# Gate values by indexed one-word transfers into a DRAM table, and a new order of the expert products

## The reference, cut to what matters

```
sc = q . sub_keys                          # 256 tokens, 8 heads, 2 halves, 128 keys
v1,i1 = top16(sc[half 0]);  v2,i2 = top16(sc[half 1])
top_s, pos = top16(v1[a] + v2[b])          # 16 experts of 16384 for a token and head
idx = i1[a]*128 + i2[b];  g = softmax(top_s)
out[t] = sum over 8*16 chosen experts k of  g[t,k] * gelu(x[t] . u[idx]) * v[idx]
```

## Time and profile before

| | us |
|---|---|
| device time, median of 2 runs | 1510.88 (1507.37 and 1514.4) |
| profiled execution: device time | 1509.89 |
| profiled execution: span, first to last instruction | 1508.1 |
| PE busy | 1470.0 (97%) |
| DVE / ACT / POOL busy | 889.2 / 819.0 / 576.4 |
| moved from and to HBM | 242.50 MB read, 7.34 MB written |

### The profile page before, as it was taken

How to read it: one execution, slowest core, us unless ns; L and a number is a source line. 1 busy time by engine, 2 the same in 40 slices (tenths; PEclk the granted TensorE clock), 3 DMA queues, 4 the chain that set the end, 5 groups by cost and what they waited for, 6 DMA issues and landing times.

```text
span 1508.1 us, 24377 instructions
## 1 busy us (share of the span) xinstructions
PE 1470.0 (97%) x8923; PEld 1302.1 (86%) x8923; DVE 889.2 (59%) x2185; ACT 819.0 (54%) x1483; POOL 576.4 (38%) x200
## 2 busy tenths in 40 slices
PE   7999999999999999989999999999999999999998
PEld 6788888788889898889999998888888888887886
DVE  4935259388336431225996662666666666667776
ACT  5556454488456644443556664555555555555554
POOL 6881665700467477456888884000000000000000
PEclk9999999999999999999999999999999999999999
DMA  8740435600334335333665334555555555556774
GB/s 332 274 169 29 167 129 177 225 30 2 108 121 163 140 141 183 121 143 113 197 211 153 98 105 161 196 195 194 185 185 189 193 195 195 186 189 219 243 241 163
DMA packets 60125, 251.08 MB, mean 166 GB/s; under 512 B 6144, under 2 KB 18560, under 8 KB 44160
## 3 DMA queue, kind: packets, MB, share of 16 engines
q1 hardware_dynamic: 60032, 249.86, 47.9%
HBM read 242.50 MB, written 7.34 MB: 166 GB/s over the span
## 4 chain that ended last, share of the span: by engine, by line
PE 66%; POOL 2%; ACT 2%; DVE 1%; issue 1%; DMA 0%; DVEq 0%; ACTq 0%
PE bank L1297 23%; PE bank L1321 9%; PE bank L702 6%; PE bank L869 6%; PE bank L1324 5%; PE bank L1250 4%; PE bank L705 3%; POOL wlo L1364 2%; PE bank L822 2%; PE bank L764 1%; PE bank L805 1%; ACT whi L1421 1%; PE bank L724 1%; PE bank L998 1%; PE bank L1150 1%; PE bank L980 1%
## 5 line engine op out<-in xcount | busy, mean ns | idle before, releaser
L1364 POOL TENSOR_TENSOR wlo<-raw,whi 128x2048 fp32r<-128x2048 f32 (+1 forms) x51 | 195.3, 3840 | 159.0 <-ACT whi L1421 158.7
L1364 POOL TENSOR_TENSOR wlo<-arena,whi 128x2048 fp32r<-128x2048 f32 (+1 forms) x45 | 195.1, 4342 | 151.1 <-ACT whi L1421 150.9
L1297 PE MATMUL bank<-whi,ghi 128*128 128x512 f32 x512 | 201.4, 393 | 3.6 <-DVE glo L2559 1.7
L1297 PE MATMUL bank<-wlo,ghi 128*128 128x512 f32 x512 | 201.0, 393 | 0.0
L1297 PE MATMUL bank<-whi,glo 128*128 128x512 f32 x512 | 200.0, 391 | 0.0
L1321 PE MATMUL bank<-hT,whi 128*128 128x512 f32 x624 | 154.3, 390 | 1.6 <-ACT whi L1767 1.6
L1321 PEld LDWEIGHTS bank<-hT,whi 128*128 128x128 f32 x624 | 117.0, 188 | 26.0 <-ACT whi L1767 1.8
L2516 DVE TENSOR_TENSOR wlo<-raw,whi 128x1024 fp32r<-128x1024 f32 x84 | 102.8, 1225 | 56.6 <-ACT whi L1774 56.6
L1377 POOL TENSOR_TENSOR wlo<-raw,whi 128x1024 fp32r<-128x1024 f32 x52 | 123.8, 2391 | 28.2 <-ACT whi L1717 28.1
L1421 ACT ACTIVATE whi<-arena 128x2048 fp32r<-128x2048 f32 x41 | 78.4, 1915 | 94.4 <-PE bank L822 28.7
L822 PE MATMUL bank<-whi,hT 128*128 128x512 f32 x512 | 125.8, 393 | 0.0
(11 more groups left out here) (336 smaller groups left out, 3027.0 us busy)
## 6 DMA issues: line engine op xcount, KB each, us to landing
raw<-ex_in SPq DMA_DIRECT2D x52, 1024.0 KB, 4.8
raw<-w_in SPq DMA_DIRECT2D x44, 1024.0 KB, 5.2
arena<-w_in SPq DMA_DIRECT2D x44, 1024.0 KB, 5.1
raw<-ex_in SPq DMA_DIRECT2D x84, 512.0 KB, 3.9
xw<-ex_in SPq DMA_DIRECT2D x26, 1024.0 KB, 4.7
xw<-ex_in SPq DMA_DIRECT2D x16, 512.0 KB, 4.0
arena<-spill SPq DMA_DIRECT2D x48, 128.0 KB, 3.8
spill<-gact SPq DMA_DIRECT2D x32, 128.0 KB, 3.7
```

Of the source, the lines that this page charges most:

```text
L1297: last = mm(bank[2 * t + h][:, :], g[:, j % 2, tok], w[:, b, at], start=False, stop=(final and i == 2), skip_group_check=True)
L1364: last = G.tensor_tensor(wlo[:, u % 2, at], slots[u % RING][:, at], whi[:, u % 2, at], ALU.subtract)
```

## The change

Stages 2 to 4 are replaced. No one-hot arrays, no transposes of the selection, no `spill`.

- **Table.** W lies in DRAM as `table` (128 tiles x 128 rows x 256 tokens, one fp32 word each, 16.8 MB). SP writes zeros to it with 16 transfers of 1 MB, four at a time, behind the loads of weight units 19, 45, 63 and 79.
- **Scatter.** DVE computes for each token and slot the place of its word. POOL issues, for each of the two token tiles, 128 indexed transfers of 128 words (one a partition). From slot 16 on they add to what is there, and after every 16 POOL waits until all issued have landed.
- **Units.** The work is a list of 356 units of 512 KB: `first` (the u of a tile) and `second` (the v of a tile, for one or both token halves). Tiles 0 to 99: first only. Tiles 100 to 127: each first is followed by a second of token half 0 of tile 0, 1, ..., 27. Then 72 seconds of half 0 (tiles 28 to 99). Then 25 times: one second of both halves (tiles 100 to 124) and four seconds of half 1; at the end three seconds of both halves. So the v of 100 tiles is loaded and split twice.
- **Ring.** All units share one ring of four quarters (raw, high, low). The first 16 low parts are POOL's, the others DVE's. On DVE they are put between the steps of the selection, by a count of spent time. The activations of all 128 tiles stay in SBUF; their gate values come back from the table through a ring of four.
- **Order on DVE.** Six of the eight score blocks come first, then the selection of token tile 0, then two score blocks and the selection of token tile 1. ACT's exponentials stand behind tiles 7 and 29.

```diff
-NL = 2 + XBODY * 13
-NA = N_KEYS - NL
+POOL_LOWS = 16
+MERGED = 48
+VISITS_FROM = 100
+VISITS = 100
+EXP_AT = (7, 29)
+UNITS = []
+for tile in range(N_KEYS):
+    UNITS.append(("first", tile, ()))
+    if visits_after(tile):
+        UNITS.append(("second", visits_upto(tile) - 1, (0,)))
+EARLY = VISITS
+UNITS += [("second", tile, (0,)) for tile in range(visits_upto(N_KEYS - 1), EARLY)]
+NARROW = 4
+for tile in range(EARLY, N_KEYS):
+    UNITS.append(("second", tile, (0, 1)))
+    if (tile - EARLY) * NARROW < EARLY:
+        UNITS += [("second", (tile - EARLY) * NARROW + i, (1,)) for i in range(NARROW)]
...
 SP:
+                if u in ZERO_AT:
+                    for i in range(4):
+                        sp_.dma_start(zero_rows[n], zeros_8).then_inc(zeroed, 16)
...
+            for n in range(NU):
+                if n < 4: ...
+                elif n - 4 < POOL_LOWS:
+                    sp_.wait_ge(u_lo_pool, n - 3)
+                else:
+                    sp_.wait_ge(u_lo_dve, n - 3 - POOL_LOWS)
+                sp_.dma_start(quarters[n % 4], ...).then_inc(u_loaded[n % 4], 16)
+                if n - 1 in PLACE:
+                    for t in some:
+                        sp_.wait_ge(scattered[t], 16 * SLOTS)
+                    if m >= 4:
+                        sp_.wait_ge(g_ready, m - 3)
+                    sp_.dma_start(w_ring[m % 4][:, tokens_of(m)], tiles_w[tile][:, tokens_of(m)])
...
 POOL:
+            pool.wait_ge(zeroed, 16 * 16)
+            for t in range(TT):
+                pool.wait_ge(places_ready, t + 1)
+                if t > 0:
+                    pool.wait_ge(scattered[0], 16 * SLOTS)
+                for s in range(SLOTS):
+                    if s > 0 and s % 16 == 0:
+                        pool.wait_ge(scattered[t], 16 * s)
+                    G.indirect_dma_start(table, IndirectOffsetOnAxis(ap=places[:, t, s:s + 1], axis=0),
+                                         values[:, t, s:s + 1], None, compute_op=ALU.add if s >= 16)
...
 PE:
+            for n in range(NU - 2):
+                if kind == "first":
+                    first_product(n, tile)
+                else:
+                    second_ready(n)          # waits glo_ready and the low part of v
+                    for t in some:
+                        last = out_part(n, t, False)
+                    last.then_inc(u_done, 1)
...
 ACT:
+            def unit_hi(n):
+                act.wait_ge(u_loaded[n % 4], 16 * (n // 4 + 1))
+                act.wait_ge(u_done, n - 3)
+                A(hi4[n % 4], quarters[n % 4], ACT.Copy).then_inc(u_hi, 1)
+            for n in range(NU - 2):
+                act.wait_ge(u_done, n + 1)
+                if first: copy of the second bank half (or gelu, tile < 48)
+                unit_hi(n + 4)
+                if first and tile >= MERGED: gelu, after DVE's sum
+                if n + 2 in PLACE:
+                    act_hi(PLACE[n + 2])     # ghi of unit n + 2
...
 DVE:
+            for n in range(lows[0] - 4, NU - 2):
+                if kind == "first" and tile >= MERGED:
+                    V.tensor_tensor(out, out, act_at(tile), ALU.add)
+                if n + 4 < NU:
+                    unit_lo()                # waits u_hi of unit n + 4, then 128x1024
+                if n + 2 in PLACE:
+                    act_lo(PLACE[n + 2])     # glo of unit n + 2
+                if n + 3 in PLACE:
+                    weigh(PLACE[n + 3])      # activation times gate, unit n + 3
```

More of the change, by code:

```diff
@@ L29, with visits_after, visits_upto @@
 PH = 8
-XRING = 3
-XBODY = 6
-NL = 2 + XBODY * 13
-NA = N_KEYS - NL
[L34 to L55, removed]
+SLOTS = PH * 16
+POOL_LOWS = 16
[3 more added lines that the diff above has]
+EXP_AT = (7, 29)
+def visits_after(i):
+    return 1 if i >= VISITS_FROM else 0
+def visits_upto(i):
+    return max(0, i - VISITS_FROM + 1)
+UNITS = []
[5 more added lines that the diff above has]
+UNITS += [("second", tile, (0,)) for tile in range(visits_upto(N_KEYS - 1), EARLY)]
+FIRSTS = len(UNITS)
+NARROW = 4
[3 more added lines that the diff above has]
+        UNITS += [("second", (tile - EARLY) * NARROW + i, (1,)) for i in range(NARROW)]
+NU = len(UNITS)
+SECONDS = [n for n, (kind, _, _) in enumerate(UNITS) if kind == "second"]
+PLACE = {n: m for m, n in enumerate(SECONDS)}
 SCALE = HD ** -0.5
@@ L144, in build @@
         x = xw[:, :].rearrange("p (t n) -> p t n", t=TT)
[L145 to L152, removed]
+        quarters, hi4, lo4 = ([w[:, i // 2, D * (i % 2):D * (i % 2) + D] for i in range(4)] for w in (raw, whi, wlo))
+        places = xw[:, 0:2 * SLOTS].bitcast(U32).rearrange("p (t n) -> p t n", t=TT)
+        values = xw[:, 2 * SLOTS:4 * SLOTS].rearrange("p (t n) -> p t n", t=TT)
+        expert, place, unread = (xw[:, (4 + i) * SLOTS:(5 + i) * SLOTS] for i in range(3))
+        w_ring = [xw[:, D + T * i:D + T * i + T] for i in range(4)]
+        token_u, token_f = sc8[:, 96:98].bitcast(U32), sc8[:, 98:100]
+        table = nc.dram_tensor("table", (P * N_KEYS * T, 1), FP32, kind="Internal").ap()
         slots = [raw[:, 0, :], raw[:, 1, :], arena[:, 0:UNIT], arena[:, UNIT:2 * UNIT]]
-        xslots = [raw[:, 1, :], raw[:, 0, :], xw[:, :]]
         base = 2 * UNIT
@@ L255, in build @@
         half_done, half_out = sem("half_done"), sem("half_out")
[L256 to L263, removed]
+        wt_taken = sem("wt_taken")
         out_ready, out_stored = sem("out_ready"), sem("out_stored")
@@ L1284, in act_tile @@
[L1284 to L1292 removed]
+                elif i > 2:
+                    pe.wait_ge(act_ready, i - 2)
@@ new lines, in first_product @@
+                pe.wait_ge(u_hi, n + 1)
+                out = first_bank(i)[:, :].rearrange("p (s t) -> p s t", s=2)
+                if i < MERGED:
+                    for k in range(KT):
+                        for r, rows_of_k in enumerate((hThi, hTlo)):
+                            mm(out[:, 0], h[:, k, :], rows_of_k[:, k, :], start=(k == 0 and r == 0), stop=False)
+                else:
+                    for k in range(KT):
+                        mm(out, h[:, k, :], hT2[:, :, k, :], start=(k == 0), stop=False)
@@ new lines, in first_product, with low_ready, out_part @@
+                low_ready(n)
+                for k in range(KT):
+                    last = mm(out[:, 0 if i < MERGED else 1], l[:, k, :], hThi[:, k, :], start=False, stop=(k == KT - 1))
+                last.then_inc(u_done, 1)
+            def low_ready(n):
+                by_pool, by_dve = lows_before(n + 1)
+                if by_dve:
+                    pe.wait_ge(u_lo_dve, by_dve)
+                else:
+                    pe.wait_ge(u_lo_pool, by_pool)
+            def out_part(n, t, final, columns=range(2)):
+                m = PLACE[n]
@@ new lines, in _ @@
+            for n in range(NU - 2):
+                kind, tile, some = UNITS[n]
+                if kind == "first":
[4 more added lines that the diff above has]
+                        last = out_part(n, t, False)
+                    last.then_inc(u_done, 1)
+            for n in (NU - 2, NU - 1):
+                second_ready(n)
+                if n < NU - 1:
+                    out_part(n, 0, False, (0,))
@@ new lines, in act_hi, with gelu @@
+            def act_hi(m):
+                if m < len(SECONDS):
+                    act.wait_ge(g_ready, m + 1)
+                    if m >= 2:
+                        act.wait_ge(u_done, SECONDS[m - 2] + 1)
+                    tok = tokens_of(m)
+                    A(ghi[:, m % 2, tok], act_at(UNITS[SECONDS[m]][1])[:, tok], ACT.Copy).then_inc(ghi_ready, 1)
+            def gelu(i, of):
+                A(act_at(i), of, ACT.Gelu_apprx_tanh).then_inc(act_ready, 1)
+            for n in range(4):
+                unit_hi(n)
@@ new lines, in _ @@
+            for n in range(NU - 2):
+                kind, tile, some = UNITS[n]
+                act.wait_ge(u_done, n + 1)
+                if kind == "first":
+                    if tile == 44:
+                        act.wait_ge(lo_ready, len(SPLIT_UNITS))
+                    if tile == 92:
+                        act.wait_ge(selected, 1)
+                    if tile < MERGED:
+                        gelu(tile, first_bank(tile)[:, 0:T])
+                    else:
+                        A(act_at(tile), first_bank(tile)[:, T:2 * T], ACT.Copy).then_inc(b_taken, 1)
+                unit_hi(n + 4)
+                if kind == "first" and tile >= MERGED:
+                    act.wait_ge(sum_ready, tile - MERGED + 1)
+                    gelu(tile, first_bank(tile)[:, 0:T])
+                if n + 2 in PLACE:
+                    act_hi(PLACE[n + 2])
+                if kind == "first" and tile in EXP_AT:
+                    act.wait_ge(top_ready, EXP_AT.index(tile) + 1)
+                    A(E, E, ACT.Exp).then_inc(g_exp, 1)
@@ new lines, in select @@
+                V.tensor_copy(places[:, t, :], place).then_inc(places_ready, 1)
+                spend(1.9)
```

(22 more changed lines are left out.)

478 lines of the change are left out of this document (109 added, 369 removed).

## The result

The changed kernel takes **1715.52 us** (median of two runs, 1714.24 and 1716.8) against 1510.88 before: a ratio of **1.136** (95% interval 1.1306 to 1.1415), slower. The forecast was 1574 us and its range ended at 1680. The direction was right and the size was not. The profiled execution has a span of 1714.9 us.

The account below looks back on a forecast made before the run. PE's pace was taken to bound the kernel: 723.7 before the expert layer, 704 of PE work, 138 lost to the new waits and 5.7 end make 1571.8, plus 1.8 around it, 1574 us; range 1525 to 1680.

Parts of the forecast that it names:

- the price of the indexed transfer: POOL's scatter into the table: 1.9 us or less per transfer, with no stall, 1.88 needed for token tile 0.
- The side estimate of 256 us: Scatter of one token tile, transfers one after the other at about 2.0 us fixed cost; the sum would be 1590.
- The threshold and the size of the rival: Late scatter, deciding from 1.9 us a transfer on: at 2.5 us, waits of 77 and 48, total 1699; chance 0.22.
- The start of the scatter: Token tile 0's places ready at 760, after six score blocks and one selection.
- The chain of waits: High part, low part, glo, PE in seconds: 2.11 us a half second, 4.29 a pair, 11.28 a group; 138 lost.
- The chain does not bind: Rival for half seconds and groups: DVE's floor of 1.54 us a half, PE's 8.16 a group; 1455 us; chance 0.17.
- The rate does not bind: Half seconds' v and gate loads: 280 GB/s needed, 412 and 442 seen where loads queue; cost 0.
- The firsts: First products of tiles 0 to 99: 48 at 2.88 and 52 at 2.72 us, 280 us, from 723.7 to 1003.
- Zeroing: Zero writes to the table, covered by attention: cost 0, without the cover 0 to 5 us.
- The gates' gain: PE's work in the expert layer: 75 us can go, 57 of gates and 18 of small things.
- The clock: Rival: PE at half clock in the half seconds, some 130 us more, 1706 in all; chance 0.06.
- The sum: Span 723.7 + 704 + 138 + 5.7 = 1571.8, and 1.8 around it: 1574 us.

Follow-up runs that it names:

- e4: Changed kernel with DVE's low part reading one of its two inputs from PSUM instead of SBUF (low parts wrong in value): 1641.93 us, ratio 1.0862.
- e2: e1 with glo and ghi moved forward, ahead of the low and high parts, behind second products: 1539.76 us, ratio 1.0176.
- e6: e2 with only 256 KB of the 512 KB of each v loaded: 1492.73 us, ratio 0.9880.
- e1: Changed kernel with one indexed transfer instead of 128 for each token tile: 1604.05 us, ratio 1.0612.
- e9: Changed kernel with all 128 second products whole, no halves, and all 256 indexed transfers issued: 1751.04 us, ratio 1.1606.
- e7: e1 with all 128 second products whole, so no v is loaded or split twice: 1469.21 us, ratio 0.9733.
- e5: Changed kernel with all 256 indexed transfers writing, none adding: 1605.53 us, ratio 1.0627.

## Why the prediction was wrong

- **The step that failed: the price of the indexed transfer.** "I take 1.9 or less, with no stall, since only every 16th waits for a landing and the issue is the nearer row." It was 2.50 for token tile 0 and 2.36 for tile 1. Its parts by the traces are these. 16 copies of 0.97 and 112 adds of 1.55 with 0.30 between them, undisturbed, are 20 + 207 = 227 us. Seven stops and the end, each for a landing of 1.4 to 4.8 us, and three pauses that the trace leaves unexplained are another 34 in e4 (261 in all). DVE's two-input low parts add the other 58. An SP issue was the wrong neighbour: POOL works through each indexed transfer itself. The side estimate of 256 us for one after the other lies near the 261 of e4, but by chance: it took the time for completion, and the trace has most of it as POOL's own work.
- **The threshold and the size of the rival were right.** The forecast said 240 us for token tile 0, 1.88 each, and 1699 for a transfer of 2.5. Lateness was 84.8 and 24.2 against 77 and 48. That 1699 lies within 1% of the result is in part luck, since 16 us less of waiting is set against 34 us more in the other stages. The rival had 0.22 of the chances; the interference of DVE was seen in the earlier trace rows and then valued at nothing, "beside DVE operations that are short or of the kind of the low parts". The low parts were the very thing (e4: 74 us).
- **The start of the scatter:** 770, not 760. Ten of the 85 us.
- **The chain of waits was right, and a little long.** 2.17 a half second against 2.11, 4.35 a pair against 4.29 (the first pair behind the wait took 6.76, of which 2.4 are the half clock). From PE's start to ACT's high part 1.78 us pass (1229.68 to 1231.46) where 1.57 was counted: the first matmul after a wait is followed 0.34 us later, not 0.227, and ACT starts 0.51 after the sixth matmul does, not 0.43. The rest of the loop took 2.57, not 2.65. e2 shows that the order of the lists makes it: -64 us. The groups, 11.87 steady, are 0.6 over the forecast; four half seconds of 0.07 more explain half of that, and the rest was not traced. The first took 14.35, the 2.5 more being the half clock.
- **"The chain does not bind" fell,** but its floor is not where it was put: with the order mended, loads hold 1.99 a half second (e2) and 1.54 is reached only with less to load (e6). "The rate does not bind" held for the changed kernel alone, at 262 GB/s and already 0.95 of DMA's time: outside the two gaps ACT hardly waits for a load there, and e2 waits for 126.
- **The firsts** ended 7 us late. 1.9 of it: the layer began at 725.58, not 723.70. Another 3.9: 53 merged firsts came 2.793 apart, not 2.72. e1 has the same pace, so the transfers did not make it; what did stays open.
- **Zeroing** cost little, as said: the layer began 0.2 to 3.7 us later than before in the changed kernel and e1 to e9, inside the forecast's 0 to 5, with each MB landing in 10.7. No run leaves the zeroing out, so what part of this is its own stays open. **The gates' gain was right:** 75 on paper, 41 net in e7.
- **The clock** in the expert layer was at half only around the two gaps, and behind each for about twelve matmuls (0.2 us each), not in the half seconds (1.00 in 1221 to 1376).
- **The sum:** its addends give 1571.4, not 1571.8; nothing hangs on the 0.4.

## What to carry to other kernels

An operation of which the trace shows no row should be priced by the engine that executes it, not by the engine that issues its nearest relative, and if 256 of it stand in one queue the deadline divided by the count says at once what price decides. Before indexed transfers are handed to POOL beside a busy DVE, ask what form DVE's instructions have: here the place of one operand was worth 74 us. Splitting products so that half can start early pays only while something is late (36 us here), and costs its full price (135 us) once that is mended; the mend comes first.

## What the runs showed of the hardware that was not expected

- An undisturbed indexed transfer of 128 words holds POOL for 0.95 to 0.98 us when it writes and 1.55 when it adds, with 0.30 to the next; waiting for all that are in flight costs 1.6 to 5.2 us. The 320 us of a token tile move 128 x 512 bytes, 0.07 MB.
- Beside DVE's two-input SBUF subtractions the add took 2.49, locked to their pace (2.79 apart, one a tile, in 989 to 1011); with one of the two inputs in PSUM it took 1.55 (e4). The copies lost 0.27 us a tile beside them (e5).
- Loads of 512 KB with gate loads of 64 KB between them held 293 to 306 GB/s at a DMA share of 0.88 to 0.92, where short stretches of before showed 412 and 442.
- After a wait of about 1 us at full clock, the first matmul of 512 columns is followed 0.34 us later, the others 0.23.
